# The Fourier branch on half of its spectrum, in a two-block transformer kernel on one core

## The reference, cut to what matters

```python
def fourier_mix(u):
    b, s, _ = u.shape
    ug = u.reshape(b, s, FOURIER_GROUPS, FOURIER_GROUP_DIM).astype(jnp.float32)
    f = jnp.fft.fft2(ug, axes=(1, 3), norm="ortho").real
    return f.reshape(b, s, FOURIER_WIDTH).astype(u.dtype)
...
        u_f, q_lat, kv_lat, k_rope, gate_logits = jnp.split(
            z, [SPLIT_1, SPLIT_2, SPLIT_3, SPLIT_4], axis=-1)
        y_a = fourier_mix(u_f) @ w_fourier_out[l]
        y_b = mla_attention(q_lat, kv_lat, k_rope, positions, q_norm[l], w_q_up[l],
                            kv_norm[l], w_kv_up[l]) @ w_mla_out[l]
```

## Time and profile before

| | us |
|---|---|
| median of 3 runs | 1769.57 |
| lowest and highest | 1768.77 and 1772.83 |
| the profiled execution | 1770.0 |
| its span in the profile | 1768.2 |
| mean granted PE clock | 0.994 |

### The profile page before, as it was taken

One profiled execution on the slowest core, in us unless ns is written; L12 is line 12 of the kernel. 1 busy time (PEld: TensorE's weight loads), 2 busy tenths in 40 slices (PEclk: granted clock), 3 DMA queues, 4 the chain that ended last, 5 costly groups with the idle time before them and its releaser, 6 DMA issues.

```text
span 1768.2 us, 23408 instructions
## 1 busy us (share of the span) xinstructions
PE 1740.0 (98%) x8554; PEld 1377.6 (78%) x8554; DVE 984.4 (56%) x1672; ACT 365.8 (21%) x814; POOL 1190.0 (67%) x1190
## 2 busy tenths in 40 slices
PE   8999999999999999999999999999999999999998
PEld 6888888887876788888888888877445778888887
DVE  4865446544765205465613657799874987116723
ACT  3100000012346311210000001445786110000001
POOL 4676767675665467667667768856663768767875
PEclk9999999999999999999999999998999999999999
DMA  9655466542331032455336533513000313233261
GB/s 354 218 188 186 143 199 196 164 155 66 95 91 40 25 104 88 163 175 191 125 101 202 191 117 107 123 58 97 25 25 1 95 57 109 97 96 95 95 146 69
DMA packets 247102, 215.28 MB, mean 122 GB/s; under 512 B 62881, under 2 KB 237406, under 8 KB 247006
## 3 DMA queue, kind: packets, MB, share of 16 engines
q1 hardware_dynamic: 214080, 211.18, 37.4%
q10 hardware_dynamic: 32926, 2.82, 1.2%
HBM read 209.72 MB, written 2.10 MB: 120 GB/s over the span
## 4 chain that ended last, share of the span: by engine, by line
PE 69%; POOL 13%; issue 9%; DVE 6%; DMA 1%; ACT 1%; SPq 0%; POOLq 0%; DVEq 0%; ACTq 0%
PE ps L822 18%; PE ps L823 18%; PE ps L824 18%; POOL w_lo L742 8%; POOL w_hi L737 2%; PE ps L1435 2%; POOL w_hi L736 2%; PE ps L1446 2%; PE ps L1466 2%; PE ps L1206 2%; DVE score L2470 1%; PE ps L1227 1%; PE ps L1215 1%; DMA ada<-in_ada_w 1%; DVE c L2469 1%
## 5 line engine op out<-in xcount | busy, mean ns | idle before, releaser
L742 POOL TENSOR_TENSOR w_lo<-raw,w_hi 128x512 fp32r<-128x512 f32 (+5 forms) x568 | 725.8, 1307 | 11.6
L822 PE MATMUL ps<-h_hi,w_hi 128*128 128x512 f32 x1176 | 459.6, 391 | 2.2 <-DVE h_lo L2613 1.4
L824 PE MATMUL ps<-h_hi,w_lo 128*128 128x512 f32 x1176 | 457.7, 389 | 0.0
L823 PE MATMUL ps<-h_lo,w_hi 128*128 128x512 f32 x1176 | 457.7, 389 | 0.0
L734 POOL TENSOR_TENSOR w_hi<-raw,ones 128x8 fp32r<-128x8 f32 x142 | 32.4, 228 | 430.1 <-PE ps L824 371.9
L822 PEld LDWEIGHTS ps<-h_hi,w_hi 128*128 128x128 f32 x1176 | 220.5, 188 | 53.7 <-issue 5.6
L824 PEld LDWEIGHTS ps<-h_hi,w_lo 128*128 128x128 f32 x1176 | 220.5, 188 | 46.6
L823 PEld LDWEIGHTS ps<-h_lo,w_hi 128*128 128x128 f32 x1176 | 220.6, 188 | 45.6
L2083 DVE SCALAR_TENSOR_TENSOR ps<-ada,cT,ps 128x256 f32<-128x256 f32 x312 | 152.9, 490 | 11.0
L737 POOL TENSOR_SCALAR w_hi<-raw 128x1024 fp32r<-128x1024 f32 (+3 forms) x142 | 155.0, 1092 | 0.0
L736 POOL TENSOR_SCALAR w_hi<-raw 128x1016 fp32r<-128x1016 f32 (+3 forms) x142 | 138.0, 972 | 0.0
(11 more groups left out here) (431 smaller groups left out, 2700.8 us busy)
## 6 DMA issues: line engine op xcount, KB each, us to landing
ada<-in_ada_w SPq DMA_DIRECT2D x31, 1024.0 KB, 6.8
ada<-in_w_ada SPq DMA_DIRECT2D x24, 1024.0 KB, 6.8
raw<-in_ffn_w_gate SPq DMA_DIRECT2D x22, 1024.0 KB, 5.1
raw<-in_ffn_w_up SPq DMA_DIRECT2D x22, 1024.0 KB, 5.1
raw<-in_w_in SPq DMA_DIRECT2D x16, 1024.0 KB, 5.0
raw<-in_w_up SPq DMA_DIRECT2D x16, 1024.0 KB, 5.4
...
```

The costliest lines, as they stand in the source:

```text
L742: last = pool.tensor_tensor(lo[:, c], src[:, c], hi[:, c].bitcast(F32), ALU.subtract)
L822: pe.matmul(o, wh, xh, start=start, stop=False)
L823: pe.matmul(o, wh, xl, start=False, stop=False)
L824: return pe.matmul(o, wl, xh, start=False, stop=stop)
```

## The change

Only half of the spectrum is computed. The channel transform makes channels 1 to 64 and channel 0 of each group (66 columns for 128), and the token transform tokens 0 to 256 (258 columns for 512). The modes of two groups lie side by side, so the token transform runs over two pairs of groups (`along_s(0)`, `along_s(1)`) with cosine and sine parts in two banks, and once more over the four channels 0 (`along_s_dc`, 4 weight columns). The rows k and 128-k of `w_fourier_out` are added for the cosine part and subtracted for the sine part: POOL does so in front of its split (`split_folded`), except for the sums of the second tile, which DVE makes (`sum_rows`). The output product gives an even and an odd part of 258 columns each; ACT copies the odd one to SBUF (`branch_half`), and DVE adds for token s and subtracts for token 512-s (`branch_out`). The rows 0 of `w_fourier_out` come in a DMA of their own and are multiplied at the end of each block. The positions' DMA and the rotary angles move ahead, between DVE's copies of the first products. POOL's split of `dft_d` goes to a place of its own and doesn't wait for a used tile, and neither do those of W_FO.

```diff
+    dft_d = np.zeros((P, 2 * MODES), np.float32)
+    dft_d[:, 0:HP] = np.cos(d[:, 1:HP + 1])
+    dft_d[:, HP - 1] *= 0.5
+    dft_d[:, HP] = 1
+    dft_d[:, MODES:MODES + HP - 1] = np.sin(d[:, 1:HP])
...
+    dft_s = np.zeros((5 * P, S_COLS), np.float32)
+    dft_s[0:HT, 0:HT + 1] = np.cos(s) * norm
+    dft_s[HT:T, 0:HT] = -np.sin(s[:, 0:HT]) * norm
+    dft_s[T, 0:HT + 1] = np.where(np.arange(HT + 1) % 2, -norm, norm)
...
         for j in range(2):
-            t[W_FO + j] = whole(w2d(a["w_fourier_out"])[:, :, 512 * j:512 * j + 512])
+            w = a["w_fourier_out"].rearrange("o (p u k) m -> (o p) u k m", u=2, k=P)[:, :, :, 512 * j:512 * j + 512]
+            t[W_FO + j] = [(w[p, :, 1:HP + 1], 0, 512, 0, p) for p in range(2)] + [
+                (w[p, :, P - 1:HP - 1:-1], 0, 512, 0, 2 + p) for p in range(2)], 4, 512
...
+        if n == W_DFT_D:
+            return mode_hi, mode_lo
...
+                if n in (W_FO, W_FO + 1):
+                    dst = slot(raw, n, kc, cols)[:, k0]
...
-            elif n == W_DFT_S:
+            elif n in (W_DFT_D, W_DFT_S):
                 pool.wait_ge(tile_used, W_MIX + 1)
...
+        def split_folded(n):
+
+            src, hi, lo = raw[:, n % 2], w_hi[:, n % 2], w_lo[:, n % 2]
+            pool.wait_ge(raw_in[n % 2], arrived[n])
+            pool.wait_ge(tile_used, n - 3)
+            plain = w_rows[:, n % 2]
+            for q in range(2 * (n - W_FO), 4):
+                c, m = slice(512 * q, 512 * q + 512), slice(512 * (q % 2), 512 * (q % 2) + 512)
+                last = pool.tensor_tensor(plain[:, c], src[:, m], src[:, 1024 + m.start:1024 + m.stop], ALU.add if q < 2 else ALU.subtract)
+            last.then_inc(rows_folded, 1)
+            pool.wait_ge(rows_folded, n - W_FO + 1)
+            if n > W_FO:
+                pool.wait_ge(fo_rows, 3)
+            pool.tensor_tensor(hi[:, 0:8], plain[:, 0:8], ones[:, 0:8], ALU.mult)
+            pool.tensor_scalar(hi[:, 8:1024], plain[:, 8:1024], 1.0, 1.0, ALU.mult, ALU.mult)
+            pool.tensor_scalar(hi[:, 1024:2048], plain[:, 1024:2048], 1.0, 1.0, ALU.mult, ALU.mult).then_inc(hi_done, 1)
+            pool.wait_ge(hi_done, n + 1)
+            for q in range(4):
+                c = slice(512 * q, 512 * q + 512)
+                last = pool.tensor_tensor(lo[:, c], plain[:, c], hi[:, c].bitcast(F32), ALU.subtract)
+            last.then_inc(split_done, 1)
...
             for k in range(4):
-                c = slice(P * k, P * k + P)
-                d = slice(P * (k // 2), P * (k // 2) + P)
-                last = mm3(ps[:, b, c], u_hi[:, gr, c], u_lo[:, gr, c], ch[:, d], cl[:, d], True, True)
+                c, o = slice(P * k, P * k + P), slice(P * k, P * k + MODES)
+                d = slice(MODES * (k // 2), MODES * (k // 2) + MODES)
+                last = mm3(ps[:, b, o], u_hi[:, gr, c], u_lo[:, gr, c], ch[:, d], cl[:, d], True, True)
                 if k == 2:
-                    last = mm3(ps[0:1, b, c], u_hi[:, gr, HT:HT + 1], u_lo[:, gr, HT:HT + 1], ch[:, 0:P], cl[:, 0:P], True, True)
+                    last = mm3(ps[0:1, b, o], u_hi[:, gr, HT:HT + 1], u_lo[:, gr, HT:HT + 1], ch[:, 0:MODES], cl[:, 0:MODES], True, True)
...
-        def along_s(gr):
-            if gr == 0:
+        def even_tokens(o, channels):
+
+            for k in range(2):
+                mm3(o, channels(a_hi, k), channels(a_lo, k), th[:, k, 0:HALF], tl[:, k, 0:HALF], k == 0, False)
+            return mm3(o, channels(a_hi, 2)[0:1], channels(a_lo, 2)[0:1], th[0:1, 4, 0:HALF], tl[0:1, 4, 0:HALF], False, True)
+
+        def along_s(p):
+            if p == 0:
                 pe.wait_ge(split_done, W_DFT_S + 1)
-            pe.wait_ge(win_free, g + gr + 1)
-            for k in range(4):
-                c = slice(P * k, P * k + P)
-                last = mm3(ps[:, (g + 4 + gr) % 4], a_hi[:, gr, c], a_lo[:, gr, c], th[:, k], tl[:, k], k == 0, k == 3)
-            signal(last, win_mm, gr, 4)
-
-        th, tl = slot(w_hi, W_DFT_S, 4, T), slot(w_lo, W_DFT_S, 4, T)
+            pe.wait_ge(win_free, g + 2 * p + 2)
+
+            def channels(t, k):
+                return t[:, k, P * p:P * p + P]
+
+            even_tokens(ps[:, 2 - 2 * p, 0:HALF], channels)
+            for k in (2, 3):
+                last = mm3(ps[:, 3 - 2 * p, 0:HALF], channels(a_hi, k), channels(a_lo, k), th[:, k, 0:HALF], tl[:, k, 0:HALF],
+                           k == 2, k == 3)
+            signal(last, win_mm, p, 3)
+
+        def along_s_dc():
+            pe.wait_ge(win_free, g + 5)
+            signal(even_tokens(ps[0:4, 2, 0:HALF], lambda t, k: t[:, k, 4 * HP:4 * HP + 4]), win_mm, 2, 3)
+
+        th, tl = slot(w_hi, W_DFT_S, 5, S_COLS), slot(w_lo, W_DFT_S, 5, S_COLS)
         for gr in range(3):
             along_d(gr)
         along_s(0)
         along_d(3)
-        for gr in range(1, 4):
-            along_s(gr)
-        g += 8
+        along_s(1)
+        along_s_dc()
...
             for first in (0, 2):
-                pe.wait_ge(win_free, g - 2)
-                for k in range(4):
-                    if j == 0 and first == 0 and k >= 2:
-                        pe.wait_ge(win_free, 15 + k)
-                    for m in (first, first + 1):
-                        c = slice(P * m, P * m + P)
-                        last = mm3(ps[:, (g + m - first) % 4], wh[:, k, c], wl[:, k, c], u_hi[:, k], u_lo[:, k], k == 0, k == 3)
-                        if k == 3:
-                            signal(last, win_mm, m, 4)
-                g += 2
+                pair = [(m, slice(P * m, P * m + P)) for m in (first, first + 1)]
+                pe.wait_ge(win_free, (16, 17, 19, 21)[2 * j + first // 2])
+                pe.wait_ge(l_lo_done, 5)
+                for p in range(2):
+                    for odd in range(2):
+                        for m, c in pair:
+                            o = ps[:, B_FO_ODD[m] if odd else m, 0:HALF]
+                            w = 2 * odd + p
+                            mm3(o, wh[:, w, c], wl[:, w, c], u_hi[:, 2 * p + odd, 0:HALF], u_lo[:, 2 * p + odd, 0:HALF],
+                                p == 0, odd == 1 and p == 1)
+                pe.wait_ge(win_free, 17)
+                pe.wait_ge(fo_rows, 2)
+                for m, c in pair:
+                    c = slice(512 * j + c.start, 512 * j + c.stop)
+                    last = mm3(ps[:, m, 0:HALF], dc_hi[:, c], dc_lo[:, c], a4_hi[:], a4_lo[:], False, True)
+                    signal(last, win_mm, m, 4)
...
+            else:
+                pe.wait_ge(win_free, 22 + i)
...
+        act.dma_start(pos1[:], a["positions"].broadcast_to([P, T])).then_inc(small_in, 16)
+        act.dma_start(dc_raw[:], a["w_fourier_out"].rearrange("o (g k) m -> (o g) k m", k=P)[:, 0]).then_inc(small_in, 16)
...
+            if j == 0:
+                act.wait_ge(small_in, 32)
+                act.copy(dc_hi[:], dc_raw[:]).then_inc(fo_rows, 1)
+            if j == 1:
+                sines(tab0, 0)
...
+        def along_s_high(p):
+            wait_product(act, win_mm, p, 3, W_DFT_S, before=8)
+            if p < 2:
+                act.copy(u_hi[:, 2 * p:2 * p + 2, 0:HALF], ps[:, 2 - 2 * p:4 - 2 * p, 0:HALF]).then_inc(win_hi, 1)
+            else:
+                act.copy(a4_hi[:], ps[0:4, 2, 0:HALF]).then_inc(win_hi, 1)
...
+        for p in range(1, 3):
+            along_s_high(p)
+
+        for u in range(2):
+            act.copy(tab1[:, u], tab0[:, u])
+
+        def branch_half(j):
+            wait_product(act, win_mm, j, 4, W_FO, before=10)
+            if j >= 2:
+                act.wait_ge(win_free, 17 + j - 1)
+            act.copy(sq[:, j % 2, 0:HT], ps[:, B_FO_ODD[j % 4], 0:HT]).then_inc(fo_half, 1)
+
+        for j in range(NC):
+            branch_half(j)
...
         for j in range(5):
             wait_product(dve, win_mm, j, 2, W_MIX)
             dve.tensor_copy(lat[:, j], ps[:, j % 4]).then_inc(win_free, 1)
+            if j == 0:
+                angles_turns(0, pos1[:])
+            if j == 1:
+                angles_rest(0)
+            if j == 2:
+                dve.wait_ge(fo_rows, 1)
+                dve.tensor_tensor(dc_lo[:], dc_raw[:], dc_hi[:].bitcast(F32), ALU.subtract).then_inc(fo_rows, 1)
+            if j == 3:
+                angles_tables(0, tab0)
...
-            dve.tensor_tensor(a_lo[:, j], ps[:, (10 + j) % 4], a_hi[:, j].bitcast(F32), ALU.subtract).then_inc(win_free, 1)
-
-        def along_s_low(j):
-            dve.wait_ge(win_hi, 8 + j + 1)
-            dve.tensor_tensor(u_lo[:, j], ps[:, (14 + j) % 4], u_hi[:, j].bitcast(F32), ALU.subtract).then_inc(win_free, 1)
+            dve.tensor_tensor(group_modes(a_lo, j), modes((10 + j) % 4), group_modes(a_hi, j).bitcast(F32), ALU.subtract)
+            dve.tensor_tensor(group_dc(a_lo, j), mean_column((10 + j) % 4), group_dc(a_hi, j).bitcast(F32),
+                              ALU.subtract).then_inc(win_free, 1)
+
+        def along_s_low(p):
+            dve.wait_ge(win_hi, 8 + p + 1)
```

(65 more changed lines are left out.)

101 lines of the change are left out of this document (65 added, 36 removed).

## The result

Four runs each: before 1769.66 us median (1768.77 to 1772.83), after 1783.15 (1781.14 to 1784.28). The ratio is 1.0075, 95% interval 1.0063 to 1.0087: 13.5 us slower, where I had forecast 8.7 faster. (Single executions far outside the others, 7369 us of the kernel before, 2160 of e7_root_first and 3488 of e8_all_three, are left out of every median and ratio here.) The profiled execution after has a span of 1781.2 us, 13.0 longer than before's.

What follows compares the result with a forecast made beforehand. PE, busy 98% of the span, was taken as the bound: 13.0 us spared, less waits of 2.0, 0.5 and 1.8, gives -8.7, so 1770.0 becomes 1761.3 us. Range 1759.5 to 1763 (chance 0.50); 8 in 10: 1757.5 to 1766.5.

Steps and rivals of the forecast that it cites:

- Output product, first tile: Start of the output product: PE waits 0.5 us for the copied and subtracted bank of pair 1; POOL no limit.
- to the second token pair, its wait included: Before the token transform's second pair: PE waits 2.0 us, until 470.65, for DVE's `a_lo` of group 3.
- wait for the first tile: Ahead of the output product: PE waits 0.5 us, until 474.15.
- wait for the second tile: Middle of the output product: PE waits 1.8 us, from 481.65 to 483.45, for POOL's second-tile split.
- The clock was a rival: Clock falls in the new waits; 4 to 10 us at the lower level cost 2 to 5; 1763 to 1767 us, chance 0.14.
- slower: Clock falls in the first wait and stays low through the output product into the attention; 1770 to 1777 us, chance 0.05.
- here it has dense ones: Argument against a lasting clock fall: earlier falls after waits came with small matmuls on PE, here they are dense.
- PE is spared 13.0 us: Transforms and output product: 32.7 us of matmuls leave, 19.9 come; bounds 7.3 and 15.2 us.
- the one price of 0.125 us: Estimated cost of each of the 159 258-column matmuls in token transform and output product, 19.9 us together.
- nothing should move: Ahead of the first channel transform at 460.8: earlier positions and angles fit into DVE's gaps; cost 0, at worst 2 us.
- POOL's additions, a rival of their own: POOL is the bound: additions put 7.5 us on it, slower splits lengthen waits; 1762.5 to 1767 us, chance 0.14.
- The two waits of the middle: PE waits 2.0 us ahead of the token transform's second pair and 1.8 us in the middle of the output product.

Runs made afterwards that it cites:

- e7_root_first: e4_mirror_copy with DVE's reciprocal of the latent norm moved ahead of its reading of the modulation columns (`read_mod`); 1766.93 us.
- e8_all_three: e4_mirror_copy with 128 streamed columns in the channel transform, all four second-tile row additions on POOL, and DVE's reciprocal first; 1763.6 us.
- e4_mirror_copy: Changed kernel with mirrored W_FO rows copied early to DRAM scratch by one DMA, each tile then loaded by four loads of outermost dimension 64; 1768.06 us.
- e2_whole: Changed kernel with each W_FO tile loaded whole, as before the change, so added and subtracted rows are not mirror images; 1769.25 us.
- e5_wide: e4_mirror_copy with the channel table zero-padded from 66 to 128 columns, so the channel transform's matmuls stream 128 again; 1765.49 us.

## Why the prediction was wrong

**The failing step is the loads of W_FO.** Under "Output product, first tile" I wrote "POOL is no limit: `dft_s` is there by 451.25", and let its additions follow `dft_s` without asking when the tile lands. The change turns one load of 1 MB into four of another shape. I gave these no row, no price and no rival, though the rule on the outermost dimension stands in the section of the Trainium skill named above. In the kernel before a load of 1 MB landed 5.0 us after its issue; in the changed kernel a quarter of it took 5.0. The wait of POOL was 15.65 us where I had none. The whole difference from my sum, at the first `W_KVUP` product (512.45 against 490.95, 21.5 us), by PE's timeline:

| piece | predicted | after | difference |
|---|---|---|---|
| ahead of the channel transform (rb late) | 0 | 0.84 | +0.8 |
| to the second token pair, its wait included | 9.84 | 9.17 | -0.7 |
| second pair and the four channels 0 | 3.0 | 6.2 | +3.2 |
| wait for the first tile | 0.5 | 6.34 | +5.8 |
| output product, first tile | 7.5 | 9.7 | +2.2 |
| wait for the second tile | 1.8 | 8.87 | +7.1 |
| output product, second tile | 7.5 | 10.5 | +3.0 |

The two waits, 12.9 us, are the slow loads. The three rows of work, 8.4 us, are the half clock for the most part: at full clock, in e8_all_three, the same matmuls take 3.6 us (472.07 to 475.67, where the wait of 0.80 begins) and 16.0, so some 6.8 are the clock and 1.6 are work that my sum priced too low.

**The clock was a rival (0.14) and a part of "slower" (0.05), with too small a price.** I said the falls would follow waits and cost 2 to 5 us. In e4_mirror_copy, with the loads mended, 17 us at half clock cost some 6.4: e8_all_three, which has none, is 7.1 shorter in the stretch, and its waits there sum to 2.3 in place of 3.0. And the falls need not follow a wait, as e2_whole and e7_root_first show. My argument against, "here it has dense ones", was wrong for the channel transform.

**"PE is spared 13.0 us" was too much.** Without its waits of 1.48 and 0.80 us the stretch of e8_all_three is 28.2 us of work, so 38.9 - 28.2 = 10.7 us are spared. The step at fault is the one price of 0.125 us for all 159 matmuls: the distance in a row of them is 0.12, but at each change between 128 weight rows and 1 or 4 about 0.1 us comes twice over, which makes the 120 of the output product 16.0 us in place of 15.0 and the 39 of the token transform 5.9 in place of 4.9. The padded channel transform adds the last 0.3. (The prediction also says that the rows at 348 and 512 columns lie 14 ns above the formula that it cites. At 512 it is 11: 227 for 216.)

**Ahead of 460.8 "nothing should move".** 0.8 us of wait came, and the stretch began 0.84 us late. The early angles were not it: DVE had them done, and the squares' sum ended earlier than before. What I missed is that `dft_s`, 650 KB in place of 1 MB, lands earlier, so that POOL's split, which began at 449.46 in place of 451.25, lay beside DVE's small operations. DVE's timeline before, and after:

```profile
450.23 0.39 DVE L2113 TENSOR_TENSOR mod<-mod,vec 128x32 f32<-128x32 f32 x2
```

```profile
449.99 1.45 DVE L2219 TENSOR_TENSOR mod<-mod,vec 128x32 f32<-128x32 f32 x2
...
451.68 0.75 DVE L2420 TENSOR_SCALAR fac<-mod 128x8 f32<-128x8 f32 x1
452.46 1.75 DVE L2422 RECIPROCAL rb<-std 128x256 f32<-128x256 f32 x1
```

e7_root_first took the reciprocal out of that queue and gained 1.1 us. It fits the lock on the shared port pair that the prediction cites from the Trainium skill ("SBUF — State Buffer", section "Who interferes with whom"); the trace agrees, 0.39 us with POOL idle against 1.45 beside it, but no run moved POOL's split away to test it. I applied it to `ln_lo` and not here.

**Right.** POOL's additions, a rival of their own, did not bound the time: with the loads mended PE waits for POOL once, 1.48 us, where I had 1.8. 258-column matmuls of one kind come 0.12 us apart at full clock. The channel transform keeps its length, 1.44 to 1.52 us a group. The two waits of the middle, 2.0 and 1.8 predicted, are 2.21 and 1.46 in e5_wide. The second tile's split takes 7.2 us, and the shift stays to the end. That the stretch of e8_all_three, 30.45 us, is so near the forecast of 490.95 - 460.81 = 30.14 is luck: 2.3 us more work than forecast, and 2.0 us less waiting (2.3 for 4.3), in a kernel with two more edits than the mended loads and the padding.
